# One smaller first slot in the down projections, an earlier inverse root, and a later rounding of the first weight slot

## The reference

```python
def s5_mixer(u, ..., w_glu):
    ...                                    # states by a scan, y per chunk
    y = jax.nn.gelu(y).astype(u.dtype)
    val, gate = jnp.split(y @ w_glu, 2, axis=-1)
    return val * jax.nn.sigmoid(gate)

def swiglu(h, w_gate_up, w_down):          # D_FF = 2816 = 22 * 128
    gate, up = jnp.split(h @ w_gate_up, 2, axis=-1)
    return (jax.nn.silu(gate) * up) @ w_down

def hybrid_mixer(h, w_in, g_group, sinks, w_out, rel_table):
    ...
    groups = []
    for y in (ya, yb, yc, yd):
        groups.append(y * lax.rsqrt(jnp.mean(y * y, axis=-1, keepdims=True) + NORM_EPS))
    y = jnp.concatenate(groups, axis=-1) * g_group.astype(jnp.float32)
    return y.astype(h.dtype) @ w_out
```

## Time and profile before

| | before |
|---|---|
| median of 3 runs | 1996.37 us (1996.29 to 1997.42) |
| the profiled execution | 1996.37 us, span 1994.6 us |
| PE busy | 1909.3 us, 96% of the span |
| DVE / ACT / POOL busy | 766.4 / 749.7 / 848.5 us |
| matmul lines on the chain that ended last | PE 87% |
| mean granted TensorE clock | 0.983 of full |

### The profile page before, as it was taken

One profiled execution on the slowest core, in us unless ns is written; L12 is line 12 of the kernel. 1 busy time (PEld: TensorE's weight loads), 2 busy tenths in 40 slices (PEclk: granted clock), 3 DMA queues, 4 the chain that ended last, 5 costly groups with the idle time before them and its releaser, 6 DMA issues.

```text
span 1994.6 us, 25043 instructions
## 1 busy us (share of the span) xinstructions
PE 1909.3 (96%) x9679; PEld 1542.6 (77%) x9679; DVE 766.4 (38%) x1292; ACT 749.7 (38%) x1160; POOL 848.5 (43%) x417
## 2 busy tenths in 40 slices
PE   2899999999999999999999999999998999999998
PEld 2677888888888868667888888888775768888887
DVE  7984231111002378882311110020636556503621
ACT  5534342232223244683422221243448362212212
POOL 1002443444444558654434444444335444434443
PEclk8799999999999899899999999999999999999999
DMA  5014233333332212102333323333420313233331
GB/s 126 13 25 139 85 85 105 89 100 95 100 101 70 85 64 85 64 2 64 85 105 84 105 83 107 108 107 96 132 74 2 95 43 105 85 105 90 100 106 63
DMA packets 210348, 168.29 MB, mean 84 GB/s; under 512 B 19537, under 2 KB 175641, under 8 KB 210200
## 3 DMA queue, kind: packets, MB, share of 16 engines
q1 hardware_dynamic: 207120, 162.05, 27.7%
q10 hardware_dynamic: 3144, 5.08, 0.8%
HBM read 162.63 MB, written 2.13 MB: 83 GB/s over the span
## 4 chain that ended last, share of the span: by engine, by line
PE 87%; DVE 5%; ACT 3%; issue 2%; POOL 1%; SPq 1%; DMA 1%; POOLq 0%; DVEq 0%; ACTq 0%
PE PS L2039 75%; PE PS L2304 2%; PE PS L2295 2%; PE PS L2314 1%; PE PS L1943 1%; PE PS L1944 1%; PE PS L2103 1%; DVE taken L1829 1%; POOL w_lo L623 1%; ACT probs_t L1141 1%; PE PS L1964 1%; PE PS L1976 1%; ACT w_hi L848 0%; SPq L473 0%; ACT probs L1130 0%
## 5 line engine op out<-in xcount | busy, mean ns | idle before, releaser
L623 POOL TENSOR_TENSOR w_lo<-raw,w_hi 128x2048 fp32r<-128x2048 f32 x147 | 679.7, 4624 | 974.3 <-ACT w_hi L848 841.7
L848 ACT ACTIVATE w_hi<-raw 128x2048 fp32r<-128x2048 f32 x147 | 281.6, 1916 | 644.3 <-PE PS L2039 644.2
L2039 PE MATMUL PS<-xT_hi,w_hi 128*128 128x512 f32 (+1 forms) x1152 | 441.1, 383 | 1.5 <-DVE xT_lo L1537 1.1
L2039 PE MATMUL PS<-xT_lo,w_hi 128*128 128x512 f32 (+1 forms) x1152 | 438.2, 380 | 0.0
L2039 PE MATMUL PS<-xT_hi,w_lo 128*128 128x512 f32 (+1 forms) x1152 | 438.2, 380 | 0.0
L2039 PEld LDWEIGHTS PS<-xT_hi,w_hi 128*128 128x128 f32 x1152 | 216.6, 188 | 46.8 <-issue 6.4
L2039 PEld LDWEIGHTS PS<-xT_lo,w_hi 128*128 128x128 f32 x1152 | 216.6, 188 | 41.8
L2039 PEld LDWEIGHTS PS<-xT_hi,w_lo 128*128 128x128 f32 x1152 | 216.7, 188 | 40.5
L2039 PE MATMUL PS<-w_hi,hT_hi 128*128 128x512 f32 x608 | 236.9, 390 | 0.0
L2039 PE MATMUL PS<-w_hi,hT_lo 128*128 128x512 f32 x608 | 236.6, 389 | 0.0
L2039 PE MATMUL PS<-w_lo,hT_hi 128*128 128x512 f32 x608 | 236.6, 389 | 0.0
(11 more groups left out here) (337 smaller groups left out, 2085.5 us busy)
## 6 DMA issues: line engine op xcount, KB each, us to landing
raw<-in_ffn_w_gate_up SPq DMA_DIRECT2D x88, 512.0 KB, 4.9
raw<-in_ffn_w_down SPq DMA_DIRECT2D x40, 512.0 KB, 4.4
raw<-in_w_up SPq DMA_DIRECT2D x32, 512.0 KB, 4.8
raw<-in_w_down SPq DMA_DIRECT2D x32, 512.0 KB, 4.5
raw<-in_dsa_w_in SPq DMA_DIRECT2D x28, 512.0 KB, 4.2
raw<-in_w_in SPq DMA_DIRECT2D x21, 512.0 KB, 4.3
raw<-in_s_w_glu SPq DMA_DIRECT2D x16, 512.0 KB, 4.5
raw<-in_dsa_w_o SPq DMA_DIRECT2D x8, 512.0 KB, 4.3
```

The costliest lines, as they stand in the source:

```text
L623: pool.tensor_tensor(w_lo[:, par, :], raw[:, par, :], f32(w_hi[:, par, :]), ALU.subtract).then_inc(w_split, 1)
L848: act.activation(w_hi[:, par, :], raw[:, par, :], ACT.Copy).then_inc(w_rounded, 1)
L2039: ins = mm(o, a if weights_stay else c, c if weights_stay else a, start=first and n == 0, stop=last and n == 2)
```

## The change

Three edits:

1. `FFN_DOWN` holds 2, 4, 4, 4, 4, 4 rows and no longer 3, 3, 4, 4, 4, 4. Both panels of both SwiGLU stages follow it.
2. In the output projection of the hybrid mixer, POOL waits for `grp_sq` and forms the inverse roots ahead of splitting slot 110, and no longer behind it.
3. ACT rounds slot 0 behind the first four `turn_hi`, and no longer ahead of the last `states_out`. `round_slot` moves down in the file with it; as it stands there it does the same.

```diff
-FFN_DOWN = [3, 3, 4, 4, 4, 4]
+FFN_DOWN = [2, 4, 4, 4, 4, 4]
...
             split_run(HIN_SLOT + 3, HOUT_SLOT - HIN_SLOT - 2)
             invert_columns(soft_units, SOFT_UNIT)
-            split_run(HOUT_SLOT + 1, 1)
             pool.wait_ge(grp_sq, 1)
             rsqrt(rstd[:, 16:32], ssq[:, 16:32], 16, 1.0 / 256).then_inc(grp_rstd, 1)
+            split_run(HOUT_SLOT + 1, 1)
             split_run(HOUT_SLOT + 2, 3)
...
                 gelu(b)
-            act.wait_ge(s5_v, NB)
-            round_slot(0, 0, 1)
             states_out(NB - 1)
...
             turn_hi(0, 4, view=chunk_view)
+            act.wait_ge(s5_v, NB)
+            round_run(0, 1)
             gelu(NB - 1)
             turn_hi(0, KT, view=chunk_view, k0=4)
             round_run(1, 1)
```

More of the change, by code:

```diff
@@ L842, in table @@
                 act.activation(tab_c[:, gs, :], tab_c[:, gs, :], ACT.Square, scale=2.0 ** 0.5).then_inc(s5_half_sin, 1)
[L844 to L848, removed]
             in_map_out(0)
@@ L878, in turn_hi, with round_slot @@
                     act.activation(o, i, ACT.Copy, scale=1.0 if gain is None else gains[:, gain * KT + k:gain * KT + k + 1]).then_inc(x_hi_done, 1)
+            def round_slot(g, par, use):
+                act.wait_ge(w_raw[par], use * 32)
+                if not isinstance(g, int) or g >= 2:
+                    act.wait_ge(w_used, g - 1)
+                act.activation(w_hi[:, par, :], raw[:, par, :], ACT.Copy).then_inc(w_rounded, 1)
             def round_run(g0, n):
```

## The result

The changed kernel takes 2013.15 us (median of 6 runs, 2009.63 to 2016.43) against 1996.33 us for the kernel before on the same chip: 16.8 us more, a ratio of 1.0087 with a 95% interval of [1.0072, 1.0102]. Forecast were 15.0 us more, 2011.4 us in a range of 2006.5 to 2016.5. The profiled execution of it took 2015.07 us with a span of 2013.3 us, 18.7 us more than the span before.

The account below looks back on a forecast made before the run. The prediction took PE's matmuls to bound the kernel (87% of the chain of waits). It added 4.5 + 6.2 + 3.0 + 1.3 = 15.0 us to 1996.4, giving 2011.4 us, range 2006.5 to 2016.5.

Parts of the forecast that it names:

- The price of readying a slot: Any weight slot: usable by PE 6.62 us after ACT begins its rounding, 4.64 us after POOL begins its split.
- Edit 3: End of the S5 stage: slot 0 is usable later and nothing comes forward, 4.47 us of delay, counted as 4.5.
- Edit 1: Second slot of each down panel: PE waits 1.43 or 1.48 us plus 0.10 for the restart, 6.2 us in all.
- Edit 2: Output projection: roots come no sooner, PE waits 2.86 us plus 0.10 at slot 110, counted as 3.0 us.
- The clock at slot 0: PE's standstill from about 176 to 180.9 lowers the clock, so 7 matmuls run slowly: 1.3 us, bounds 0 and 5.1.
- The like case of the earlier trace: Granted clock was 0.50 from 831.56 to 841.80, read as following a stretch in which PE waited again and again.
- disagrees: At 731.5 the trace was said to contradict the skill's rule: 2.50 us with next to no PE work, clock at 1.00.
- The clock falls more often: Rival, chance 0.20: further clock loss at slot 110, around 660 and at slot 0, 20 us more in all, 2016.5 us.

Follow-up runs that it names:

- e1_down: Edit 1 alone, FFN_DOWN = [2, 4, 4, 4, 4, 4], on the kernel before: 2005.06 us, ratio 1.0049.
- e9_after_wide: The changed kernel (all three edits) with the matmuls of 72 columns widened to 128: 2007.88 us, ratio 1.0059 to the kernel before.
- e12_wide_down: The kernel before with its matmuls of 72 columns widened to 128, plus edit 1: 1994.87 us, ratio 0.9992 to the kernel before.
- e5_down_second: The kernel before with FFN_DOWN = [4, 2, 4, 4, 4, 4], the small slot second in each down panel: 2003.44 us, ratio 1.0038.
- e8_sums: Edit 2 with PE's sums of squares and their transposes one output-projection step earlier each: 1999.51 us, ratio 1.0013 to the kernel before.
- e3_round0: Edit 3 alone, slot 0 rounded behind the first four high copies, on the kernel before: 2003.38 us, ratio 1.0036.
- e7_fill: Edit 3 alone, plus four PE matmuls of 384 columns of constants behind the last S5 transposes: 2002.16 us, ratio 1.0039 to the kernel before.
- e6_round0_mid: The kernel before with slot 0 rounded behind the last copy of the states, ahead of the first four high copies: 1999.61 us, ratio 1.0023.
- e2_roots: Edit 2 alone, the inverse roots ahead of the split of slot 110, on the kernel before: 2003.50 us, ratio 1.0039.
- e11_wide_roots: The kernel before with its matmuls of 72 columns widened to 128, plus edit 2: 1993.46 us, ratio 0.9991 to the kernel before.
- e10_wide_fill: The kernel before with 72-column matmuls widened to 128, plus matmuls of constants in the selected-key attention's first waits: 1986.57 us, ratio 0.9956.

## Why the prediction was right

- **The price of readying a slot.** 6.62 us from the rounding's start, from the one wait before. After: slot 0 is rounded from 171.20 and used at 177.91, 6.71; slot 110 is used 4.63 after its split began, against 4.64 taken. At the down panels it is 4.75 (515.05, the split's start, to 519.80), 0.11 more; the first matmul there waits for the hidden units as well as for the split, but that this makes the difference isn't shown.
- **Edit 3.** 4.47 forecast, 4.32 measured, and 4.31 alone. That nothing comes forward was right: ACT's idle time took it all.
- **Edit 1.** 6.2 forecast, 6.6 measured, in four places and again in three other kernels (e1_down, e9_after_wide, e12_wide_down). The wait was put at 1.43 to 1.48 and was 1.34 to 1.40 in the table; the restart was put at 0.10 and is the rest up to 1.62 to 1.68. Most of that rest is a matter of counting: the table's 1.34 us begin at the end of the last matmul (518.46), but at 0.227 us each the next would have begun at 518.30. The mechanism stands on e5_down_second: a slot with 5.4 us of work leaves the next one late wherever it stands.
- **Edit 2.** 2.96 forecast, 2.93 measured. The roots waited for the sums and not for the split; e8_sums showed it by moving the sums.
- **The clock at slot 0.** 1.3 forecast, 2.05 measured. The term was mis-sized since 10 matmuls of slot 0 (the x10 of its row), and not 7, began at the lower level, until 182.33; in e3_round0 and e9_after_wide it was 1.5 and 1.6 us. That there would be a fall was right, but not for the reason given, the 4.5 us with hardly any work. In e3_round0, e7_fill and e9_after_wide the clock fell during the last transposes, before PE could stand waiting for the split, and in e6_round0_mid, where PE hardly waited, it fell too and cost some 1.2 us. So this term came out partly by luck, and what the wait alone does stays open. The like case of the earlier trace rows was also read too broadly. Just ahead of 831.56 PE had waited for 0.90 us and was in a wait of 1.57; the longer one of 2.07 us came behind the fall:

```profile
829.24 1.14 PE L2295 MATMUL PS<-kT,qT 64*128 64x128 f32 x8 [0.90 <-ACT kT L1022]
831.94 1.49 PE L2295 MATMUL PS<-kT,qT 64*128 64x256 f32 x4 [1.57 <-DVE neg_max L1749]
835.50 0.66 PE L2304 MATMUL PS<-ident,probs 128*128 128x128 f32 x2 [2.07 <-DVE probs L1759]
```

  The Trainium skill (page "TensorE: Matmul & The Clock Gate", section "HAM oscillation — how this bites in real kernels") puts such falls down to waits between bursts of matmuls, in its example waits of some 3 to 5 us for transfers. The falls just named came behind shorter waits than these. The 2.50 us at 731.5 and the 2.62 us at slot 110, which brought none, are shorter too, so that the prediction's "disagrees" goes too far.
- **The rivals.** "The clock falls more often" was named with 0.20, at slot 110 and around 660. The second came in part (17.07 us instead of 13.65, 1.65 us), though the change need not be its cause, as the stretch is as long in kernels that change nothing ahead of it. The first did not come at the wait but 53 us behind it, in the cross attention; in e9_after_wide it came at the wait as well. Single edits came out 3 to 5 us over their waits, and added up (1.24%, 25 us by the ratios) they are more than the whole (0.87%). Since the waits are the same to some 0.1 us in every kernel, except at slot 0 (2.8 to 3.1), the difference lies elsewhere, in the profiles in these short stretches; with the widest of them removed, edit 1 fell back to its waits, and edit 2 to within 2 us of its own. What brings them is open. It isn't only which execution was profiled: all five runs of e2_roots have a mean granted clock of 0.979 to 0.981, and ten of the eleven runs of the kernel before beside them have 0.981 to 0.984.
- **How near the sum came.** The four terms measured 4.3, 6.6, 2.9 and 2.05 us, 15.9 against the 15.0 forecast. The other places of the table above (5.6 us) and the start (2.8 us less) were in no term, and that they partly cancel is luck.

The time from start to states was 166.05 us in one profiled execution (e11_wide_roots) and 169.87 in another, the kernel before, which has the longest of all fourteen. It may be part of the spread of single runs of the kernel before, 1992.5 to 2001.8.

## What to carry to other kernels

Where several engines ready weights for PE in turn, the time to ready one slot is a fixed price; compare it with the work in the slot ahead, and don't make any slot smaller than that (5.4 us of work against 6.6 us here). Before an operation is put ahead of another on an in-order engine, read what it waits for: one that waits for a later event brings nothing forward and holds back all that is queued behind it. And look at the granted clock in stretches of dense but narrow matmuls: one cost 6.4 us here, as much as the four new waits of the down panels together, and no table of waits shows it.

## What the runs showed of the hardware

- Matmuls of 128 columns were issued at the same 0.11 us as those of 72. In all five kernels that have them the clock stayed at its full level through the stretch, where in all nine with the narrow ones it was down for 13.65 to 20.48 us: 6.4 us of 1996 won for computing more. In one of the five (e10_wide_fill) it fell for 3.41 us just behind the stretch.
- The clock fell in transposes of 64 columns between which PE was never idle for more than 0.34 us (e6_round0_mid). Behind a wait of 2.6 us at slot 110, with full-width matmuls on either side, it stayed up in three kernels and fell at once in a fourth (e9_after_wide, 8 matmuls at the lower level). The length of the wait alone doesn't tell.
